# Second mixer: the values' projection as two pairs of weight chunks, seven half-size products each

## The reference

```python
def hybrid_mixer_2(h, w_in, conv_w, conv_b, dt_bias, a_log, d_skip, ssm_norm_g, w_out, rel_table):
    z, xbc, dt_raw, q, k, v = jnp.split(h @ w_in, HY_SPLITS, axis=-1)
    xbc = jax.nn.silu(causal_depthwise_conv(xbc, conv_w, conv_b))
    ...
    y = ssd_chunked(xs, dt, A, bm.reshape(b_, s, SSM_GROUPS, SSM_STATE), cm.reshape(b_, s, SSM_GROUPS, SSM_STATE))
    ...
    att = dilated_attention(q.reshape(b_, s, ATT_GROUPS, ATT_KV_HEADS, ATT_HEAD_DIM),
                            k.reshape(b_, s, ATT_KV_HEADS, ATT_HEAD_DIM),
                            v.reshape(b_, s, ATT_KV_HEADS, ATT_HEAD_DIM), rel_table)
    return jnp.concatenate([y, att.astype(y.dtype)], axis=-1) @ w_out
```

## Time and profile before

| | |
|---|---|
| time, median of 3 runs | 1464.32 us (1462.7 to 1465.55) |
| span of the profiled execution, first to last instruction | 1458.9 us |
| its own time beside the span | only the span is on the page; the median of the runs is 5.4 us above it |
| busy over the span | PE 1373.3 us (94%), DVE 873.2 (60%), ACT 252.0 (17%), POOL 258.8 (18%) |
| granted TensorE clock, mean | 0.982 of full speed |
| chunks 0 to 39 on PE | from 481.5 us to 825.1 us |
| chunks 16 to 19 (values) on PE | from 605.09 us to 642.5 us |

### The profile page before, as it was taken

The page is one execution under the profiler, slowest core; times in us unless marked ns, Lnnn a source line. Parts: engine busy times, 40 slices in busy tenths (PEclk is TensorE's granted clock), DMA queues, the critical chain, the costliest instruction groups (busy, mean ns, idle before and its releaser), DMA issues. The chain is left out here.

```text
span 1458.9 us, 18939 instructions
## 1 busy us (share of the span) xinstructions
PE 1373.3 (94%) x7533; PEld 1013.0 (69%) x7533; DVE 873.2 (60%) x1502; ACT 252.0 (17%) x540; POOL 258.8 (18%) x342
## 2 busy tenths in 40 slices
PE   5999999887766999999999999999999999999997
PEld 1877655554433788868888888777776878888843
DVE  2458685442222668763454685788763874777864
ACT  2221121000001211222345101000002113211101
POOL 5078010000000200453355402100020100000000
PEclk9999999998998999999999999999999999999999
DMA  9976878999999598856774455898864552555531
GB/s 350 319 258 229 283 307 347 363 416 415 417 418 378 181 316 277 298 162 164 161 179 132 158 163 175 326 336 311 303 230 141 155 157 80 163 164 171 172 129 46
DMA packets 176055, 355.57 MB, mean 244 GB/s; under 512 B 7289, under 2 KB 137040, under 8 KB 158560
## 3 DMA queue, kind: packets, MB, share of 16 engines
q1 hardware_dynamic: 166720, 313.64, 60.6%
q0 software_dynamic: 9248, 40.71, 9.5%
HBM read 352.58 MB, written 1.74 MB: 243 GB/s over the span
## 5 line engine op out<-in xcount | busy, mean ns | idle before, releaser
L1824 PE MATMUL PS<-HT,ring 128*128 128x256 f32 x1152 | 258.3, 382 | 0.1
L1824 PEld LDWEIGHTS PS<-HT,ring 128*128 128x128 f32 x1152 | 215.4, 190 | 36.0 <-issue 7.9
L1542 DVE TENSOR_TENSOR X<-X,PS 128x1024 f32<-128x1024 f32 x14 | 17.1, 1221 | 112.0 <-PE PS L1318 112.0
L1265 PE MATMUL PS<-ring_extra,slot_rows 128*32 128x256 f32 x576 | 55.2, 440 | 27.7 <-DMA ring_extra<-in_expert_w_gate 7.0
L2758 PE MATMUL PS<-HT,ring 128*128 128x256 f32 x352 | 76.8, 379 | 0.0
L2787 PE MATMUL PS<-ada_stage,half_sums 128*128 128x256 f32 x320 | 75.6, 379 | 0.0
L2787 PE MATMUL PS<-ring,half_sums 128*128 128x256 f32 x320 | 75.6, 379 | 0.0
L2758 PEld LDWEIGHTS PS<-HT,ring 128*128 128x128 f32 x352 | 66.7, 190 | 9.0
L2764 PE MATMUL PS<-ring,hid 128*128 128x512 f32 x160 | 71.8, 592 | 0.0
L2787 PE MATMUL PS<-ring,HT 128*128 128x256 f32 x304 | 68.8, 379 | 0.0
L2787 PEld LDWEIGHTS PS<-ring,half_sums 128*128 128x128 f32 x320 | 59.4, 190 | 11.2 <-issue 4.3
(11 more groups left out here) (713 smaller groups left out, 2450.5 us busy)
## 6 DMA issues: line engine op xcount, KB each, us to landing
ring<-in_hy_w_in SPq DMA_DIRECT2D x40, 1024.0 KB, 7.5
ring_extra<-in_w_ada SPq DMA_DIRECT2D x24, 1024.0 KB, 8.0
ada_stage<-in_ada_w POOLq DMA_DIRECT2D x24, 1024.0 KB, 7.4
ring<-in_ffn_w_gate SPq DMA_DIRECT2D x22, 1024.0 KB, 5.8
ring<-in_ffn_w_up SPq DMA_DIRECT2D x22, 1024.0 KB, 5.7
ring<-in_ffn_w_down SPq DMA_DIRECT2D x22, 1024.0 KB, 6.0
ring_extra<-in_expert_w_down SPq DMA_DIRECT2D x18, 1024.0 KB, 22.9
ring_extra<-in_expert_w_up SPq DMA_DIRECT2D x18, 1024.0 KB, 20.1
```

The lines of the kernel that those rows point to most:

```text
L1265: mm = pe.matmul(PS[e * SLOTS:(e + 1) * SLOTS, 2, j * CW:(j + 1) * CW], hs[:, k, e * SLOTS:(e + 1) * SLOTS], w[e][:, k, :], start=(k == 0) ...
L1542: dve.tensor_tensor(part, part, PS[:, 6:8, :], ALU.add).then_inc(added, 1)
L1824: mm = pe.matmul(dst, w[:, k, half * P:(half + 1) * P], HT[:, k, :], start=(k == 0), stop=(k == KT - 1))
```

## The change

The four chunks of the values become two pairs (16 and 17, 18 and 19). In a pair the product of `h` (two halves of tokens by two halves of inputs) with 512 columns (two halves of inputs by two chunks) is formed from seven products of halves, P1 to P7, in place of eight, with the sums of Winograd's form of Strassen's method, the same scheme as the output projection's. Per pair PE has seven groups of four products of 128 x 128 by 128 x 256, in the order `V_ORDER`, one at each quarter, and nothing of its own at the eighth, (17, 3) and (19, 3). New on DVE: four half sums of HT (`v_half`, 128 x 512, at (8, 3) to (11, 3)), four sums of weights for a pair (`v_sum`, 128 x 1024, at the places in `v_sum_at`), seven joins for a pair (`v_join`, 128 x 256, operands in PSUM and in V). ACT copies P1 of each pair into V in place of the four evacuations. A pair's products lie in three banks of PSUM, 2, 3 and 6 or 0, 1 and 7, and in a pair P7 takes the place of P2. The half sums lie in `b_c`, whose former content is used up by then, the sums in `out_sums`, `rx_zb` and the ring's own slot. The two slots of a pair are freed by P7 and P4. Chunks 20 and 21 wait for the last join (`v_joined` 6). Some semaphores of earlier stages are used on, with their counts so far added to the waits (`small`, `cum_in`, `bias_in`); this moves no instruction.

```diff
+        V_ORDER = ("P2", "P1", "P3", "P5", "P6", "P7", "P4")
+        V_BANKS = ((2, 3, 6), (0, 1, 7))
+        V_HOMES = {"P2": (0, 0), "P1": (0, 1), "P3": (1, 0), "P5": (1, 1), "P6": (2, 0), "P7": (0, 0), "P4": (2, 1)}
+        v_half_at = {(8 + j, 3): j for j in range(4)}
+        v_sum_at = {(14, 3): (0, 0), (15, 1): (0, 1), (15, 2): (0, 2), (15, 3): (0, 3),
+                    (16, 1): (1, 0), (17, 2): (1, 1), (17, 3): (1, 2), (18, 1): (1, 3)}
+        v_join_at = {(V0 + 2 * pair + at // 4, at % 4): (pair, at) for pair in range(2) for at in (3, 5, 6, 7)}
...
+                def v_seventh(pair, at):
...
+                    if name == "P5":
+                        pe.wait_ge(v_summed, 4 + 4 * pair + 1)
+                    if name == "P6":
+                        pe.wait_ge(xready, SSM_IN // CW)
+                        pe.wait_ge(v_summed, 4 + 4 * pair + 2)
+                    if name == "P7":
+                        pe.wait_ge(v_summed, 4 + 4 * pair + 4)
+                        pe.wait_ge(v_joined, 3 * pair + 1)
+                    if name == "P4":
+                        pe.wait_ge(v_joined, 3 * pair + 2)
...
+                    for k in range(4):
+                        mm = pe.matmul(v_home(pair, name), lhs[:, k, :], rhs[:, k, :], start=(k == 0), stop=(k == 3))
+                    mm.then_inc(used if name in ("P7", "P4") else v_products, 1)
...
+                    if V0 <= s < Q0:
+                        pair, at = v_product(s, q)
+                        if at < len(V_ORDER):
+                            v_seventh(pair, at)
...
+                            if s in (Q0, Q0 + 1):
+                                pe.wait_ge(v_joined, 6)
...
-                    elif s < Q0:
-                        j = s - V0
-                        ins = act.activation(V[:, :, j * CW:(j + 1) * CW], rows, ACT.Copy)
...
+                        act.wait_ge(v_products, v_done(pair, "P1"))
+                        act.activation(V[:, 1, 2 * pair * CW:(2 * pair + 1) * CW], v_home(pair, "P1"), ACT.Copy)\
+                            .then_inc(v_moved, 1)
...
+                def v_half(j):
...
+                    dve.tensor_tensor(v_halves[:, at], in0, in1, op).then_inc(v_summed, 1)
...
+                def v_sum(pair, j):
...
+                    out, in0, in1 = ((t1, w1[:, 0:4, :], w0[:, 0:4, :]), (t2, w1[:, 4:8, :], t1),
+                                     (w1[:, 0:4, :], w1[:, 4:8, :], w1[:, 0:4, :]), (t4, w0[:, 4:8, :], t2))[j]
+                    dve.tensor_tensor(out, in0, in1, ALU.subtract).then_inc(v_summed, 1)
...
+                def v_join(pair, at):
+                    v00, v01, v10, v11 = (V[:, i, (2 * pair + h) * CW:(2 * pair + h + 1) * CW] for i in range(TT) for h in range(2))
+                    if at == 3:
+                        dve.wait_ge(v_moved, pair + 1)
+                        dve.tensor_tensor(v00, v_home(pair, "P2"), v10, ALU.add).then_inc(v_joined, 1)
+                    if at == 5:
+                        dve.wait_ge(v_products, v_done(pair, "P6"))
+                        dve.tensor_tensor(v11, v_home(pair, "P6"), v10, ALU.add).then_inc(v_joined, 1)
+                        dve.wait_ge(v_joined, 3 * pair + 2)
+                        step(dve.tensor_tensor(v01, v_home(pair, "P5"), v11, ALU.add))
+                        step(dve.tensor_tensor(v01, v_home(pair, "P3"), v01, ALU.add))
+                    if at == 6:
+                        dve.wait_ge(used, base + V0 + 2 * pair + 1)
+                        step(dve.tensor_tensor(v10, v_home(pair, "P7"), v11, ALU.add))
+                        step(dve.tensor_tensor(v11, v_home(pair, "P5"), v10, ALU.add))
+                    if at == 7:
+                        dve.wait_ge(used, base + V0 + 2 * pair + 2)
+                        dve.tensor_tensor(v10, v_home(pair, "P4"), v10, ALU.add).then_inc(v_joined, 1)
...
                     if (s, q) in add_at:
                         add(add_at[s, q])
+                    if (s, q) in v_half_at:
+                        v_half(v_half_at[s, q])
+                    if (s, q) in v_sum_at:
+                        v_sum(*v_sum_at[s, q])
+                    if (s, q) in v_join_at:
+                        v_join(*v_join_at[s, q])
```

93 lines of the change are left out of this document (70 added, 23 removed).

## The result

The changed kernel is slower: 1471.51 us in the median (1467.9 to 1477.53, 13 runs) against 1463.73 for the kernel before (1460.11 to 1469.77, 13 runs), ratio 1.0056 with a 95% interval of 1.0041 to 1.0072. That is 8.2 us more (6.0 to 10.5), where 4.1 were forecast. The time lies just beyond the upper end of the range.

The account below looks back on a forecast made before the run. PE was taken as the bound, at clock 1.00 without waits; 7.5 us late, less 3.46 saved, plus about 0.1 for PE's restart gave +4.1 us, 1468.4 us against a median of 1464.32; range 1462.3 to 1471.5.

Parts of the forecast that it names:

- Saved 3.46 us: PE in the values' chunks: 8 of 64 products go, 0.432 us each, 3.46 us less.
- half sums: DVE in chunks 8 to 11: four of 0.69 us each, covered by a 1.30 us fetch wait, costing nothing.
- the signs that I named: PE idle before values(1), (3), (7) and P7; DVE without fetch idle, chunks 15 to 17; sums 1.2 to 2.2 us.
- A clock below 1.00 between 610 and 650: TensorE in the values' chunks: a clock fall there was listed as showing the main case wrong.
- The 0.1 for PE's new start after a wait: PE restarting after waiting for W in the values' chunks: about 0.1 us added to the sum.
- the 5.4 us outside the span: Whole program: median run 1464.32 us, 5.4 outside the profiled span of 1458.9, added to reach the forecast time.
- Joins: DVE, fourteen at 0.42 us, seven ahead of head 15: lateness 8.4 if all lost, 5.5 if free; taken as partly lost.
- 7.5 late: PE at values(7), waiting for W(15) behind DVE's queued sums and joins: its whole lateness, 7.5 us.
- the 0.4 at values(1): PE at values(1): one sum of 1.22 us delays W(3) to 602.9 against 602.46, 0.4 us late.
- The rival of the clock: TensorE's clock falls after waits before values(3) and values(7): up to 2.5 us more, about 1471; chance 0.10.
- PE has no wait later that would give it back: PE after the values' chunks: full to the mixer's end, so the +4.1 us stays in the total.
- The rival of the hidden sums: DVE's sums run while POOL works, hiding 5.2 us: -1.3 to -0.2 us, 1463 to 1464.1; hidden or half hidden, chance 0.25.

Follow-up runs that it names:

- no_sums: Changed kernel without its eight sums of weights, half sums, seven products and joins kept; ratio 0.9989 to before, values(0) to first score product 73.79 us.
- fill kernels: Two versions of the changed kernel with idle PE products ahead of values(3) and values(7), 7 and 4 or 7 and 8; ratios to before 1.0033 and 1.0053.
- changed_again: Changed kernel profiled a second time without an edit; no median of its own, values(0) to first score product 82.79 us.
- fill_more: Changed kernel with 7 idle PE products ahead of values(3) and 8 ahead of values(7); ratio 1.0053 to before.
- sums_psum: Changed kernel with one operand of each sum of weights from a PSUM bank at rest in place of the ring; ratio 1.0020 to before.

## Why the prediction was wrong, point by point

**Saved 3.46 us, half sums, ring loads, ACT:** right. Without the sums the stretch is 73.79 = 77.25 - 3.46. Of the signs that I named, PE's waits for `ssm_weights`, DVE without an idle for a fetch and sums of up to 2.02 us came; the wait before P7 did not, in the changed kernel. A clock below 1.00 between 610 and 650, named as a sign of being wrong, came as well. The 0.1 for PE's new start after a wait had no row behind it, but it was right: in the changed kernel W(15) takes 2.21 from 636.58 and ends at 638.79, and values(7) starts at 638.93. The lateness in the table is counted between starts of PE and holds these 0.14. Nor are the 5.4 us outside the span a fixed part: the runs that have both times are 1.7 to 2.0 apart (the changed kernel 1473.73 and 1472.0), so before's profile was one of its shorter executions; the sum, which is a difference, is not touched by it.

**Joins:** I took them as partly lost. By themselves they are free (no_sums: 1.1 us of margin left, what the saved quarter leaves of 2.9), and putting off most of pair 0's gave 0.27 us. No run takes the joins alone away beside all eight sums, so what they cost there stays open. The row that I weighed against (a DVE instruction that reads PSUM beside two W, unhindered) was the better guide.

**The step that failed first: the size of "7.5 late".** It is 8.67 and 8.99 in the two profiles. The part behind values(1) came out nearly right: 7.54 and 7.14, against 7.5 - 0.4 = 7.1. That is partly luck, since two errors cancel in it. From values(1) to values(3) the lateness grew by 3.74 and 3.73 us where 3.1 - 0.4 = 2.7 were forecast (no join stands there yet), and from values(3) to values(7) by 3.80 and 3.41 where 7.5 - 3.1 = 4.4 were.

The term that was off is the 0.4 at values(1), which was 1.13 and 1.85. I had added one sum to W(3) of the one profile that I had, in which the addition of (14, 3) starts 0.95 us ahead of values(0). Where it stands is not fixed: -0.27 us in the changed kernel, +0.44 in its second profile, -1.10 and +0.32 in the fill kernels (start of the addition less start of values(0)), and the lateness of values(1) is that number plus 1.41, to 0.01, in all four. Additions follow their own chain of fetches, about 7.3 us each, and PE its chunks. The work behind values(1) adds to that lateness: values(7) stands 36.98, 36.58, 36.99 and 37.01 us behind values(0) and that lateness in the four.

More profiles of before would not have warned me: its three have -0.95, -1.33 and -1.18. In two of the four a slow transfer made most of the difference: from the issue of the fetch for the addition of (10, 3) to the addition's start it was 6.3 us in changed_again (issued at 566.27) and 6.2 in fill_more, and 4.9 to 5.4 in the three of before and in the other two. DVE stood idle for that fetch, 2.08 and 1.96 us, so neither a half sum nor PE held it up. Why these fetches were slow is not known.

**The rival of the clock** had 0.10, because "no wait expected here is as long as 4.38". The forecast had two waits of over 2 us in it, and the runs show falls after 3.32 and 2.10. What it cost was mis-sized too: not a fall for each wait but only the last one, 0 to 1.70 us, because time lost to the clock ahead of W(15) is time that PE would have waited.

**"PE has no wait later that would give it back"** looked only at waits that give time back. A later wait could also come up anew, and one did: 2.0 us in the third block, the one term that no rival had.

**The rival of the hidden sums:** wrong. They don't run beside W; sums_psum shows that about 5 us come from that. The rival's 5.2, priced from the blocked differences, is another quantity, and I take the closeness for chance.

The sum as it is now: lateness 8.67 or 8.99, saved 3.46, clock 1.70 or 0, third block 2.0, together 8.9 and 7.5 us; the runs give 8.2 (6.0 to 10.5). By these two profiles, of the forecast's shortfall of 4.1 us, 2.0 are the third block, 1.2 to 1.5 the lateness, for the most part by the place of the additions, and the rest the clock.

**Left open:** why the new projection shifts the third block's weights. Before, DVE waited 1.53 us there for a load (`ring<-in_ffn_w_up`, the first row of before's third block above) and so came later to the additions; after, the load was in time and the addition met POOL's products. The order and the time of issue are not the reason. SP's rows of before, then of the changed kernel:

```profile
1050.03 0.54 SPq L251 DMA_DIRECT2D ring<-in_ffn_w_up  x1
```

```profile
1061.10 0.54 SPq L251 DMA_DIRECT2D ring<-in_ffn_w_up  x1
```

Both stand 141.31 us behind the start of that second group of products on `HT` (908.72 and 919.79), and so they do in all fourteen profiles to 0.01 us. It is the transfer that differs: 10.3 to 11.8 us from issue to landing in the five profiles without the wait, 8.0 to 8.2 in the nine with it. What shortens it behind the new projection is not known. Chunk 0 started at 479.5 to 484.8 us in the profiles, with the same program ahead of it, the latest two in the changed kernel; that too is not explained, and I count it as chance.

## What to carry to other kernels

Before work is put on an engine with "free" time, ask which of its instructions shut out its neighbour: here a DVE sum with two SBUF operands beside POOL's products cost three times what the queue's length says (7.5 us of lateness for the eight, and 2.5 with one operand of each from PSUM). A sum put right behind the differences does not stand clear of W either, because W comes an exponential later. When a wait is forecast where two chains of different period meet, give their meeting a spread: it moved by 1.5 us among four profiles here, and by 0.4 in the three of before. Price the clock behind the last wait of a row of waits only. A product saved on the bound engine is worth its time only if the engines behind it have margin at each place where it waits for them: in this stage 2.9 us, of which the saved products took 1.7 before the first sum.
